# Post-norm layers with MoE on one core: the mean's sum over z tiles moved to VectorE, one modulation row moved behind the squares

## What is computed

```
mod = silu(cond) @ w_mod[l] + b_mod[l]          # 6 x 1024 values per kind of token
x = layer_norm(ALPHA * x + gate1 * y, ln1_g, ln1_b)      # y: token mixer
u = x * (1 + scale2) + shift2
x = layer_norm(ALPHA * x + gate2 * hier_moe(u, p), ln2_g, ln2_b)
layer_norm: mu = mean(x); var = mean((x - mu)**2); (x - mu) * rsqrt(var + eps) * g + b
```

## Time and profile before

| | |
|---|---|
| median of 3 runs | 1164.38 us (1163.55 to 1166.48) |
| the profiled execution | 1162.57 us, its span 1160.8 us |
| TensorE matmul, busy | 963.8 us (83% of the span) |
| VectorE, busy | 373.2 us (32%) |
| ScalarE, busy | 232.2 us (20%) |
| mean granted clock of TensorE | 0.94 of full speed |

### The profile page before, as it was taken

One profiled execution on the slowest core, in us unless ns is written; L12 is line 12 of the kernel. 1 busy time (PEld: TensorE's weight loads), 2 busy tenths in 40 slices (PEclk: granted clock), 3 DMA queues, 4 the chain that ended last, 5 costly groups with the idle time before them and its releaser, 6 DMA issues.

```text
span 1160.8 us, 14048 instructions
## 1 busy us (share of the span) xinstructions
PE 963.8 (83%) x5338; PEld 564.9 (49%) x5338; DVE 373.2 (32%) x901; ACT 232.2 (20%) x567; POOL 181.2 (16%) x217
## 2 busy tenths in 40 slices
PE   4899998985998865998989988997699986779882
PEld 2456455543555433553455545554455553445442
DVE  0168561165111111112437845126411110111232
ACT  1200264051111100111120036305111110111112
POOL 5000000003222231220020000000333223223000
PEclk8899989995999997999999999999699998989996
DMA  9962261275999999988594227048699998999601
GB/s 349 388 261 109 69 255 58 108 315 217 402 412 416 413 411 414 411 332 325 190 356 151 109 91 290 1 157 331 226 400 411 415 414 350 401 411 411 257 1 54
DMA packets 73136, 321.88 MB, mean 277 GB/s; under 512 B 13150, under 2 KB 17590, under 8 KB 48752
## 3 DMA queue, kind: packets, MB, share of 16 engines
q1 hardware_dynamic: 57824, 294.14, 63.8%
q0 software_dynamic: 15248, 26.87, 6.3%
HBM read 321.46 MB, written 23.59 MB: 297 GB/s over the span
## 4 chain that ended last, share of the span: by engine, by line
PE 68%; DMA 12%; DVE 9%; SPq 5%; ACT 3%; issue 2%; POOLq 0%; DVEq 0%; POOL 0%; ACTq 0%
PE ps L1058 15%; PE ps L824 13%; PE ps L1073 9%; PE ps L1006 7%; DMA ring<-in_w_up 5%; PE ps L827 4%; DMA ring<-in_w_in 3%; PE ps L1066 2%; DMA arena<-u_rows,row_idx 2%; PE ps L993 2%; PE ps L984 2%; SPq L567 2%; PE ps L786 2%; SPq L562 1%; DVE xT L1662 1%
## 5 line engine op out<-in xcount | busy, mean ns | idle before, releaser
L1058 PE MATMUL ps<-ring,tail 128*64 128x256 f32 x1760 | 207.0, 383 | 7.4 <-DMA ring<-in_w_up 5.6
L1058 PEld LDWEIGHTS ps<-ring,tail 128*64 128x64 f32 x1760 | 146.5, 138 | 76.9 <-issue 27.5
L824 PE MATMUL ps<-uT,ring 128*128 128x384 f32 x448 | 151.4, 496 | 4.7 <-ACT uT L1218 2.6
L1793 DVE TENSOR_TENSOR arena<-arena,ps 128x128 f32<-128x128 f32 x68 | 19.5, 287 | 366.0 <-ACT arena L1368 366.0
L824 PEld LDWEIGHTS ps<-uT,ring 128*128 128x128 f32 x448 | 86.3, 194 | 62.2 <-issue 5.8
L1073 PE MATMUL ps<-ring,krow 128*64 128x512 f32 x408 | 104.9, 634 | 4.0 <-issue 2.1
L1368 ACT ACTIVATE arena<-ps 128x128 f32<-128x128 f32 x68 | 18.9, 278 | 426.7 <-PE ps L1058 406.6
L683 POOL DMA_INDIRECT y_pairs<-tail,row_idx x56 | 56.4, 1008 | 281.7 <-PE ps L1066 230.3
L678 POOL DMA_INDIRECT arena<-u_rows,row_idx x66 | 69.4, 1052 | 50.2 <-issue 31.9
L1066 PE MATMUL ps<-cst,arena 128*128 128x128 f32 x272 | 42.7, 287 | 34.7 <-DMA arena<-u_rows,row_idx 30.9
L1518 DVE SCALAR_TENSOR_TENSOR arena<-arena,dw 128x414 f32<-128x414 f32 x118 | 67.6, 645 | 0.0
(11 more groups left out here) (268 smaller groups left out, 1046.9 us busy)
## 6 DMA issues: line engine op xcount, KB each, us to landing
ring<-in_w_gate SPq DMA_DIRECT2D x55, 1024.0 KB
ring<-in_w_up SPq DMA_DIRECT2D x55, 1024.0 KB
ring<-in_w_down SPq DMA_DIRECT2D x55, 1024.0 KB
ring<-in_w_mod SPq DMA_DIRECT2D x12, 3072.0 KB, 11.1
arena<-in_w_gate SPq DMA_DIRECT2D x13, 1024.0 KB
arena<-in_w_up SPq DMA_DIRECT2D x13, 1024.0 KB
arena<-in_w_down SPq DMA_DIRECT2D x13, 1024.0 KB
ring<-in_w_mod SPq DMA_DIRECT2D x6, 2048.0 KB, 16.3
```

What stands on the lines that cost most here:

```text
L824: last = mm(ps[:, n % 4, 0:T], slot[s][:, k, c:c + P], uT[:, k, :], start=(k == 0), stop=(k == KD - 1))
L1058: last = mm(ps[W * half:W * (half + 1), b, 0:2 * P].rearrange("p (j f) -> p j f", j=2), xc[:, b, k, :], gate_up_w[s][:, :, k, half * P:(ha ...
```

## The change

VectorE adds z tiles 0 to 6 together itself: after the z of each tile m from 1 to 6 it waits for its own `z_ready`, from the second addition on also for its own last addition, and adds the tile into `ln_t[:, 0]`, which is free until the reciprocal goes there. The sixth addition raises `z_summed`. TensorE then makes two products with ones for the mean in place of eight: one of the sum, when `z_summed` is raised, and one of tile 7. `layer_norm` is called once per norm, behind all eight branch tiles. In norm 2 of layer 0 two modulation rows stand ahead of the squares in place of three, and six behind them in place of five. The two semaphores for the mean and for the squares become one, `norm_sums`, which is raised twice per norm.

```diff
-                def layer_norm(which, n):
-
-                    wait(z_ready, l, which * KD + n + 1)
-                    last = mm(ps[:, 4, 0:T], C["ones"], uT[:, n, :], start=(n == 0), stop=(n == KD - 1))
-                    if n == KD - 1:
-                        last.then_inc(mean_ready.sem, 1)
-                        if which == 0:
-                            mod_product(l, 2, 7, range(2))
-                        elif l + 1 < DEPTH:
-                            mod_product(l + 1, 0, 7, range(MOD_K))
-                        for m in range(KD):
-                            wait(squared, l, which * KD + m + 1)
-                            last = mm(ps[:, 5, 0:T], C["ones"], ln_t[:, 2 + m, :], start=(m == 0), stop=(m == KD - 1))
-                        last.then_inc(sq_used.sem, 1)
+                def layer_norm(which):
+
+                    wait(z_summed, l, which + 1)
+                    mm(ps[:, 4, 0:T], C["ones"], ln_t[:, 0, :], start=True, stop=False)
+                    wait(z_ready, l, which * KD + KD)
+                    mm(ps[:, 4, 0:T], C["ones"], uT[:, KD - 1, :], start=False, stop=True).then_inc(norm_sums.sem, 1)
+                    if which == 0:
+                        mod_product(l, 2, 7, range(2))
+                    elif l + 1 < DEPTH:
+                        mod_product(l + 1, 0, 7, range(2))
+                    for m in range(KD):
+                        wait(squared, l, which * KD + m + 1)
+                        last = mm(ps[:, 5, 0:T], C["ones"], ln_t[:, 2 + m, :], start=(m == 0), stop=(m == KD - 1))
+                    last.then_inc(norm_sums.sem, 1)
...
-                    if m >= 1:
-                        layer_norm(0, m - 1)
-                layer_norm(0, KD - 1)
+                layer_norm(0)
...
-                    if m >= 1:
-                        layer_norm(1, m - 1)
-                layer_norm(1, KD - 1)
+                layer_norm(1)
                 if l + 1 < DEPTH:
-                    mod_product(l + 1, 0, 7, range(MOD_K, KD))
+                    mod_product(l + 1, 0, 7, range(2, KD))
                     mod_turn(l + 1, 0, 6, 0)
...
                         last.then_inc(z_ready.sem, 1)
-                    wait(mean_ready, l, which + 1)
+                        if 1 <= m < KD - 1:
+                            wait(z_ready, l, o + m + 1)
+                            if m > 1:
+                                after(own.n)
+                            add = v.tensor_tensor(ln_t[:, 0, :], uT[:, 0, :] if m == 1 else ln_t[:, 0, :], uT[:, m, :], ALU.add)
+                            if m < KD - 2:
+                                own.add(add)
+                            else:
+                                add.then_inc(z_summed.sem, 1)
+                    wait(norm_sums, l, 2 * which + 1)
```

More of the change, by code:

```diff
@@ L178, in check @@
         assert self.n == self.raised.per_layer, (self.raised.sem, self.n, self.raised.per_layer)
-DVE_STEPS = 200
+DVE_STEPS = 210
 def build(nc, g, consts, lam_dram, u_rows, y_pairs, y_prompt, y_sample, new_k, new_v):
@@ L398, in build @@
         z_ready = signal("z_ready", 2 * KD)
-        mean_ready = signal("mean_ready", 2)
+        norm_sums = signal("norm_mean_then_squares", 4)
+        z_summed = signal("z_tiles_summed", 2)
         centred = signal("centred", 2 * KD)
         squared = signal("squared", 2 * KD)
-        sq_used = signal("squares_summed", 2)
         root_ready = signal("root_ready", 2)
@@ L1333, in squares_root @@
                         fn(ln_t[:, 2 + m, :], uT[:, m, :], ACT.Square).then_inc(squared.sem, 1)
-                    wait(sq_used, l, which + 1)
+                    wait(norm_sums, l, 2 * which + 2)
                     fn(ln_t[:, 1, :], ps[:, 5, 0:T], ACT.Sqrt, bias=epsc[:], scale=1.0 / D).then_inc(root_ready.sem, 1)
```

## The result

The changed kernel took 1149.19 us (median of 4 runs, 1143.76 to 1151.84) against 1165.03 us before (4 runs, 1163.55 to 1166.48): ratio 0.9858, 95% interval 0.9819 to 0.9897. Its profiled execution took 1148.44 us. Four runs don't fix the size, so I ran it twice more. Over all 16 of its runs the mean is 1148.6 us (standard deviation 3.9, so 1.0 of the mean), over 98 runs of the kernel before 1163.8: a gain of **15.2 us, give or take 2**, where 12.1 were forecast. The changed kernel also spreads more (1143.2 to 1154.8) than the one before (standard deviation 2.3).

What follows compares the result with a forecast made beforehand. TensorE, two thirds of the chain of waits, was taken as the main bound. Gains of 7.74 + 3.90 + 0.5 = 12.1 us took the median 1164.38 to 1152.3 us; own range 1150.3 to 1154.6, full range 1149.5 to 1156.5.

Steps and rivals of the forecast that it cites:

- Norm 1: Output tiles of norm 1: six ones products fewer at 0.645 us, additions hidden; 3.87 us per layer, 7.74 us.
- Norm 2, the turns: Norm 2, tiles 0 to 3: three ones products leave the TensorE-VectorE turns, 0.65 us each; 1.95 us per norm.
- Tiles 4 to 7: Norm 2: VectorE becomes the bound, steps stay at 1.31 us; 0 us, between +0.15 and -0.3 us per norm.
- the forecast's best bound: Norm 2, tiles 4 to 7: 1.26 us per step if the next z starts before the addition is shown as ended.
- The modulation row: Layer 0, norm 2: squares' sum done 0.86 us earlier, then the turn is late next; gain 0.5 us, bounds 0.3 and 0.86.
- The clock: Norm 2: rival that idle time between products of tiles 4 to 7 drops TensorE's clock, 1170.3 us; chance 0.03.
- The rival's own 18 us: Loss if TensorE's clock halves in each norm 2: 12.8 us in layer 0, 5.2 in layer 1; chance 0.03.
- So the stream moves as a whole: Experts' stream behind norm 1: its loads are released earlier too, so norm 1's 7.74 us reach the end.
- The terms' bounds: Whole kernel: the terms' lower and upper bounds give gains of 11.3 to 12.8 us.
- additions that cost more on VectorE: Norm 2: rival, three exposed additions cost 0.3 us more each, norm 2 gives 1.05 us; 1154.1 us, chance 0.08.
- a stream that does not move: Experts' stream: rival, norm 1's 7.74 us lost, 1160.0 us; in one layer alone 1156.2; chance 0.06 together.
- no effect: Whole kernel: rival, gains eaten by differences in how the transfers meet; 1164 us, chance 0.02.

Runs made afterwards that it cites:

- norm1_doubled: Kernel before, with the ones products of tiles 0 to 5 of norm 1 made twice, the second time unread: 1171.26 us, ratio 1.0067.
- row_only: Kernel before, with only the modulation row moved behind the squares: 1162.95 us, ratio 0.9988.
- the padded kernel: Changed kernel with 24 tiny unread products in TensorE's wait for its first weights, restoring its program's length: 1151.96 us, ratio 0.9907.
- experiment 2: Changed kernel with TensorE's idle time ahead of norm 2's sum filled, by unread products (1148.89 us) or partly by useful modulation rows (1145.57 us).
- rows_and_filler: Changed kernel with layer 0's modulation rows 0 and 1 ahead of norm 2's sum, row 2 behind the mean, unread products in layer 1: 1145.57 us, ratio 0.9846.
- the other filled kernel: Changed kernel with three unread ones products ahead of the sum in each norm 2: 1148.89 us, ratio 0.9871.

## Why the prediction was right and wrong

**Norm 1** (7.74 us): right. It is 3.87 us per layer in every profile with the change, and 7.3 for twelve products in norm1_doubled. VectorE's additions are hidden.

**Norm 2, the turns** (1.95 us each): right in size, 3.52 us each. **Tiles 4 to 7** (0 us): the step is 1.25 us, at the forecast's best bound (1.26), so each norm gives 0.2 us more than taken. The addition lasts 0.558 us, as the row of the same shape said; the table of the Trainium skill ("VectorE: DVE Perf Modes", "The TRN2 errata — SBUF-src ops pay a fixed extra latency per instruction") would have 0.46, and the trace disagrees with it and agrees with the formula beside the table, 0.557.

**The modulation row** (0.5 us): the mechanism is there, the turn is late next, and the squares to the projection take 0.3 us more, where the forecast had 0.86 - 0.5 = 0.36. Its size can't be told from the times: row_only is at -1.7 with an interval from -3.4 to +0.5, and both norms gave -15.2 with the row and -14.5 without.

**The clock.** The forecast took 1.00 throughout norm 2 and gave a fall 0.03. The argument against it was that tiles 4 to 7 leave gaps of less than 0.7 us. It overlooked the gap of 1.98 us ahead of the sum: with VectorE as the bound and all branch products done early (24 of L1174 in one piece of 2.94 us), TensorE's idle time gathers in one place. In layer 0 the low clock costs 1.6 us, in layer 1 up to 2.7 in some runs. The rival's own 18 us were far too many: the low stretch lasts 3.4 us in layer 0, over before the squares, and 3.4 or 6.8 in layer 1, not up to the last of them. That the loss in layer 0 is returned with 1.9 us, because the changed kernel has its full clock at layer 1's projection, was luck: the forecast did not have it, it comes only where the row is moved too, and why is open. The Trainium skill ("TensorE: Matmul & The Clock Gate", "Why this matters for your kernels") warns there of idle gaps longer than this one of 1.98 us; in the trace the shorter one was enough, in 14 of 18 norms.

**The step that failed** is "So the stream moves as a whole" in what carries the gains to the end. In layer 0 it does, to 0.1 us: the first chunk is even 1.9 us ahead of what norm 1 explains (its gate and up take 3.64 us in place of 4.63, the gather 4.17 in place of 5.02), and the DMA-bound stretch takes that back. In layer 1 it also gets 2.8 us shorter (2.4 between all ten profiles with both norms changed, the padded kernel apart, and all nine with at most one), for a reason that no row on norms or loads could show: the change shortens TensorE's program, a packet of instructions no longer passes beside the last scatter ahead of the loop, the scatter lands 1.2 us earlier, and TensorE's clock behind it is less often low. The sum had this term at nothing. With TensorE's length restored the gain is 10.9 us (interval 7.9 to 13.7), which holds the forecast's 12.1, but in part by luck, as that kernel also differs in layer 0. In the stages the argued terms come to 7.74 us in norm 1, as forecast, and to 1.1 and 1.2 us in the two layers' norm 2, where 2.45 and 1.95 were forecast and the low clock took the rest; 1.9 came at the projection and 2.8 in the stream, where nothing was forecast. These two make up the missing 3 us and what the clock cost in norm 2.

**The range** began at 1149.5 us. The terms' bounds give 1164.38 - 12.8 = 1151.6 at the lowest, 1150.8 with the spread of three runs; the prediction's 1150.3 is lower by half a us than its own working. The range assumed the changed kernel to be as steady as the one before. It isn't: its standard deviation is 3.9 us against 2.3, and a median of four can be 2 us off its mean.

The rivals: additions that cost more on VectorE, no (1.25 us); a stream that does not move, no; no effect, no.

**A version that beats both** came out of experiment 2. rows_and_filler does useful rows in the gap ahead of the sum: 1145.1 us over 11 runs, 3.5 below the changed kernel (give or take 2.4), ratios 0.9846 [0.9823, 0.9869] and 0.9839 [0.9820, 0.9859] to the kernel before. It keeps the clock up in both norms 2 and has 36.3 us for the last stage in both profiles. At layer 1's projection it pays like the other filled kernel (149.6 us).

## What to carry to other kernels

Work that leaves the engine that sets the pace is worth its full length, and can be counted product by product, if the engine it goes to has idle time in each step. Where the pace then passes to the other engine, look for where the first one's idle time gathers, and put useful work there. Before calling a difference of 0.3% the effect of a change, ask whether the same number of instructions elsewhere does it too: pad the program and see.

## What the hardware showed that was not expected

- The landing time of an indirect DMA at a fixed place in the program went with the place of TensorE's instruction packets: 7.3 to 8.0 us with a 16 KB packet beside it, 6.2 to 6.9 without, and 0.57 us more in the mean over the scatters of all chunks. The Trainium skill ("Runtime: NRT & Kernel Launch", "Instruction fetch mechanics") says that programs are refilled in blocks of 16 KiB, 256 instructions, and that crossing into the next is mostly hidden. The packets of the trace have that size and are 260 records apart. Hidden it may be for TensorE itself; the scatter beside the packet lands about 1 us later here.
- Idle time of 1.98 us behind a half-busy stretch was followed by TensorE's lower clock level in 14 of 18 norms, for 3.4 us in layer 0 and 3.4 or 6.8 us in layer 1. With the gap filled it never was (6 norms), and the low stretch was back at the projection 17 us later.
- A z (two VectorE instructions, 0.74 us together), an addition that waits for it (0.56 us) and a next z that waits for neither follow one another every 1.25 us, where the durations add up to 0.74 + 0.56 = 1.30.
